# Two attention loops of a two-block kernel: operands split once and loaded through SyncE, masks added on VectorE, and the units put in another order

## The reference, cut to what matters

```python
# window attention: 16 heads in 4 groups that share keys and values, head width 64, 128-query blocks
s_win = jnp.where(valid, einsum(qb, kb) * scale, NEG_INF)     # keys within +-128
s_ctx = einsum(qb, k_ctx) * scale                             # 256 context keys
p = softmax(concat([sink, s_ctx, s_win]))[1:]                 # a sink logit per head
out = einsum(p, concat([v_ctx, vb]));   y = (out * silu(g)) @ w_out_c

# forgetting attention: 8 heads, causal, cum = cumsum(log_sigmoid(f))
s = einsum(q_blk, k) * scale + c_blk[..., None] - cum_k
out = einsum(softmax(where(mask, s, -inf)), v)

# beside it: causal depthwise convolution of 31 taps, then layer norm and silu
u = silu(layer_norm_2(causal_depthwise_conv(u, conv_w, conv_b), g, b))
```

## Time and profile before

| | us |
|---|---|
| median of 3 runs | 2823.35 (2822.56 to 2829.22) |
| profiled execution, its own time | 2825.2 |
| its span in the profile | 2823.4 |
| TensorE busy in the span | 2456.3 (87%) |
| VectorE, GpSimd, ScalarE busy | 1486.1, 1377.5, 879.9 |
| window attention, 883 to 1230 | 347 |
| forgetting attention, 1679 to 1885 | 206 |
| mean granted TensorE clock, share of full | 0.928 |

### The profile page before, as it was taken

One profiled execution on the slowest core, in us unless ns is written; L12 is line 12 of the kernel. 1 busy time (PEld: TensorE's weight loads), 2 busy tenths in 40 slices (PEclk: granted clock), 3 DMA queues, 4 the chain that ended last, 5 costly groups with the idle time before them and its releaser, 6 DMA issues. The chain is left out here.

```text
span 2823.4 us, 32941 instructions
## 1 busy us (share of the span) xinstructions
PE 2456.3 (87%) x11695; PEld 2025.6 (72%) x11695; DVE 1486.1 (53%) x2088; ACT 879.9 (31%) x1534; POOL 1377.5 (49%) x1348
## 2 busy tenths in 40 slices
PE   6799998988998999989778946578789999999996
PEld 2688886777887888877556735467567887888874
DVE  1715636565453888846879547663862222222236
ACT  3521112133014777743323346552341000000012
POOL 2445646552424656427557835346564453333350
PEclk9899999999997989989899978879899999999997
DMA  7345434322243223133232233315222221111121
GB/s 251 127 146 149 112 109 153 138 60 105 89 150 103 86 75 98 46 118 116 59 117 66 79 134 98 97 60 194 60 78 72 68 82 45 45 48 54 53 71 60
DMA packets 146129, 273.33 MB, mean 97 GB/s; under 512 B 16236, under 2 KB 50344, under 8 KB 144688
## 3 DMA queue, kind: packets, MB, share of 16 engines
q1 hardware_dynamic: 114208, 177.65, 20.8%
q10 hardware_dynamic: 31760, 93.57, 9.0%
HBM read 224.99 MB, written 46.17 MB: 96 GB/s over the span
## 5 line engine op out<-in xcount | busy, mean ns | idle before, releaser
L807 POOL TENSOR_SCALAR WH<-RAW 128x512 fp32r<-128x512 f32 (+1 forms) x470 | 345.7, 735 | 1017.7 <-PE PS L920 892.5
L918 PE MATMUL PS<-HXH,WH 128*128 128x512 f32 (+1 forms) x1904 | 762.0, 400 | 87.0 <-DVE XX L2170 23.1
L919 PE MATMUL PS<-HXL,WH 128*128 128x512 f32 (+1 forms) x1904 | 751.7, 395 | 0.0
L920 PE MATMUL PS<-HXH,WL 128*128 128x512 f32 (+1 forms) x1904 | 750.8, 394 | 0.0
L810 POOL TENSOR_TENSOR WL<-RAW,WH 128x512 fp32r<-128x512 f32 (+1 forms) x470 | 644.8, 1372 | 39.2
L918 PEld LDWEIGHTS PS<-HXH,WH 128*128 128x128 f32 (+1 forms) x1904 | 363.3, 191 | 177.0 <-DVE XX L2170 23.7
L919 PEld LDWEIGHTS PS<-HXL,WH 128*128 128x128 f32 (+1 forms) x1904 | 363.4, 191 | 79.1 <-issue 2.7
L920 PEld LDWEIGHTS PS<-HXH,WL 128*128 128x128 f32 (+1 forms) x1904 | 362.3, 190 | 79.4
L2209 DVE TENSOR_TENSOR TM<-PS,TM 128x512 f32<-128x512 f32 x44 | 28.4, 686 | 378.7 <-ACT TM L1625 378.6
L1625 ACT ACTIVATE TM<-PS 128x512 f32<-128x512 f32 x44 | 23.9, 595 | 552.1 <-PE PS L920 552.1
L895 POOL TENSOR_SCALAR PB<-PB,RC 128x640 f32<-128x640 f32 (+1 forms) x128 | 99.7, 779 | 159.3 <-DVE RC L2400 159.1
(11 more groups left out here) (281 smaller groups left out, 4519.0 us busy)
## 6 DMA issues: line engine op xcount, KB each, us to landing
RAW<-in_ada_w SPq DMA_DIRECT2D x160, 256.0 KB, 2.7
RAW<-in_w_ffn_in SPq DMA_DIRECT2D x224, 128.0 KB, 2.1
RAW<-in_w_in_ab SPq DMA_DIRECT2D x88, 256.0 KB, 2.7
RAW<-in_w_in SPq DMA_DIRECT2D x56, 256.0 KB, 2.7
RAW<-in_w_ffn_out SPq DMA_DIRECT2D x52, 256.0 KB, 2.6
XR<-XX ACTq DMA_DIRECT2D x3, 4096.0 KB, 12.1
XX<-XR ACTq DMA_DIRECT2D x3, 4096.0 KB, 14.0
RAW<-in_w_in_c SPq DMA_DIRECT2D x40, 256.0 KB, 2.7
```

The source lines that it names most:

```text
L807: g.tensor_scalar(WH[:, sw, 0:m], RAW[:, r, 0:m], 1.0, 0.0, ALU.mult, ALU.add).then_inc(gpsimd_done, 1)
L918: mm(out, wh, xh, start=first, stop=False, **kw)
L919: mm(out, wh, xl, start=False, stop=False, **kw)
L920: return mm(out, wl, xh, start=False, stop=last, **kw)
```

## The change: what it does

1. **Operands are split once, where they are made.** After a `q` projection of the first block VectorE writes the rotated queries to `RX`, ScalarE the high part, VectorE the low part, and ScalarE's queue stores both (`QXD`, two stores where there was one). The same is done for `q2`, `k2` and `v2` with `SPH` and `SPL`; there a PSUM bank is now free when VectorE's low part has been taken, not after ScalarE's copy. VectorE's list has these subtractions between the parts of the convolution.
2. **SyncE loads the parts ready for use** in `beside(n)`, between the slots of its list: per block of window attention eight loads of queries (2 MB, each half of the partitions written twice) and one of the gate; per head of the forgetting attention six loads of queries and keys (1.5 MB), the decay row (0.5 MB) and the values (0.5 MB). All `prep` functions go.
3. **Window masks on VectorE.** The extreme and the mask are one instruction (scores plus mask to `PB`, line 2454), ScalarE's exponential works in place on `PB`, the two mask matmuls go, the sink's column is written once per group and head, and scores wait for the extreme of unit u-2, not for the exponential.
4. **Another order.** `AT` says at which unit a tile is transposed, `PV_AT`, `OTT_AT` and `OTA_AT` when a step's product, copy and sum run; VectorE takes the low parts a unit later, ahead of that unit's extreme, and the reciprocal after it; GpSimd's `ada_tile` stands after heads 3 and 0 and not after 0 and 1.
5. **The layer norm's tail** (reciprocal in four pieces, multiplications, `Silu`, store) moves into `attf`, between its units 5 and 22.

```diff
+CONV_TAIL = (5, 7, 9, 11, 13, 15, 17, 19, 22)
+        AT = {"c": {5: [5, 5, 6, 6, 7], 4: [5, 6, 7, 7]},
+              "f": {8: [5, 5, 5, 5, 6, 6, 7, 7], 4: [6, 7, 7, 8]}}
+        PV_AT, OTT_AT, OTA_AT = {"c": 9, "f": 9}, {"c": 11, "f": 9}, {"c": 13, "f": 13}
...
+            def load_q(b):
...
+                if b >= 2:
+                    sp.wait_ge(products_done, upto("sc", "c", 16 * (b - 1) - 1))
+                for x in range(2):
+                    for half in range(2):
+                        src = QXD[x][64 * half:64 * half + 64, 2 * kv:2 * kv + 2, hf * HALF:(hf + 1) * HALF]
+                        for o_ in (slice(0, 64), slice(64, P)):
+                            sp.dma_start(QS[b % 2][x][o_, half:4:2, :].bitcast(F32), src).then_inc(rq_loaded[b % 2], 16)
...
+            def load_v(hd):
+                if hd >= 2:
+                    sp.wait_ge(products_done, upto("pv", "f", 2 * hd - 3))
+                else:
+                    for j in range(4):
+                        sp.wait_ge(split_stored[j], upto("sps", ("v2", "h1"), j))
...
+                if f == 0:
+                    load_v(0)
+                    load_qk(1)
+                    load_nb(1)
+                    load_v(1)
+                if 4 <= f < 32 and f % 4 == 2 and f // 4 < 7:
+                    load_qk(f // 4 + 1)
+                    load_nb(f // 4 + 1)
...
             for n, (kind, src, _) in enumerate(SLOTS):
+                beside(n)
...
                             if u >= 2:
-                                pe.wait_ge(scalar_done, upto("exp", "c", u - 2))
-                            pe.wait_ge(vector_done, upto("qs", s // 4, h // 2))
+                                pe.wait_ge(vector_done, upto("mx", "c", u - 2))
+                            pe.wait_ge(rq_loaded[(s // 4) % 2], upto("rql", s // 4))
...
+                            if i == 0 or (h < 2 and i in (1, 7)):
+                                sink = (PS[:, sb, p0 * P + 127:p0 * P + 128] if h < 2 else PS[:, sb + 1, 256:257])
+                                ins = mm(sink, ONF[0:1, :], NSK[0:1, hd:hd + 1], start=True, stop=True)
...
+                        for z, ti in tiles.get(u - 1, []):
+                            low(z, ti)
...
+                            v.tensor_tensor_reduce(out=PB[s % 2][:, h, lo + x:641 + x], in0=src, in1=mask[:, x:641 - lo + x],
+                                                   scale=1.0, scalar=3e38, op0=ALU.add, op1=ALU.min,
+                                                   accum_out=MX[s % 2][:, h:h + 1]).then_inc(vector_done, 1)
...
                 elif kind == "attf":
                     tiles = spread("f")
+                    for j in range(4):
+                        dve.wait_ge(split_stored[j], upto("sps", ("v2", "h1"), j))
+                    dve.wait_ge(scalar_done, upto("csd"))
```

532 lines of the change are left out of this document (270 added, 262 removed).

## The result

The changed kernel takes **2682.82 us** (median of 4, 2680.55 to 2686.06), the kernel before, run beside it, 2822.95 (2820.26 to 2829.22): ratio 0.9501, 95% interval 0.9482 to 0.9521. The forecast was 2740, range 2705 to 2778. The sign was right; the gain was 140 us and not 83. The profiled execution has a span of 2679.2 us, 144.2 less than before's 2823.4.

What follows compares the result with a forecast made beforehand. It took window attention as bound by TensorE's work and forgetting attention by a chain through ScalarE and VectorE. Terms 40 + 8 + 17 + 18 = 83 us off 2825.2 gave 2742, median 2740, range 2705 to 2778.

Steps and rivals of the forecast that it cites:

- The new order costs no instruction. [...] Both are inside the 300.: Window attention: 340 falls to 300 us, a term of 40 (0 to 70), the new order's effect included.
- VectorE busy at 81%, its share today: Window attention: VectorE's busy share stays as before in the 300 us taken for the changed loop.
- So the first loop is bound by TensorE's work: Window attention before the change: TensorE busy 93%, its summed work 336 of 340 us.
- TensorE's need: Window attention changed: TensorE's work alone takes 270 us at clock 0.92, the loop's lower bound.
- The 188 us: Forgetting attention from its first unit: 206 falls to 188 us, a term of 18, between 0 and 46.
- Ahead of window attention: Before the first window scores: queries lie ready, so scores start at about 875; term 8 us, bounds 5 and 9.
- the sign that I gave, 4 us: Ahead of window attention: first scores come 4 us after the last gate store starts, not 9.
- Convolution stage and the hole behind it: Before forgetting attention: the hole shrinks, less 2.4 us of convolution delay; term 17 us, bounds 12 and 24.
- VectorE's bound is reached: Both attention loops: window attention at 270, forgetting attention at 160, kernel 2682 us; chance 0.06.
- Only the holes close: Both loops are paced by round trips and stay as long; gain 8 + 17 = 25 us, kernel 2798; chance 0.08.
- The clock, the other side: Window attention: thinner TensorE work lowers the granted clock; at 0.60 the kernel takes 2853 us; chance 0.04.
- SyncE's list: Both loops: loads hold back modulation weights, 13 bursts of GpSimd waiting lose 139 us, kernel 2879; chance 0.03.

Runs made afterwards that it cites:

- e11: Changed kernel with the whole order undone and window scores waiting for the exponential again: 2743.98 us, window attention 299.7, forgetting attention 190.2.
- e1: Changed kernel with its new order (fourth part) undone: 2744.03 us, window attention 299.2, forgetting attention 192.3.
- e7: Changed kernel with order and scores' wait undone, TensorE's removed window work back, layer norm's tail ahead of forgetting attention: 2750.66 us, window attention 310.5.
- e2: Changed kernel with TensorE's removed window work put back (two identity matmuls and the sink in every unit): 2712.34 us, window attention 306.6.
- b1: Kernel before, without its mask matmuls and with sinks only in each group's first block: 2812.23 us, window attention 333.3.
- e10: Changed kernel with only the tables of units for tiles, products, copies and sums undone: 2722.34 us, window attention 284.4, forgetting attention 187.9.
- e4: Changed kernel with two modulation weight pieces loaded ahead of the nine loads at forgetting attention's start: 2673.09 us, forgetting attention 156.4.
- e5: Changed kernel with the layer norm's tail back ahead of forgetting attention: 2668.41 us, forgetting attention 147.6.
- e6: Changed kernel with 64 idle VectorE subtractions added in window attention, four in a row: 2752.04 us, window attention 340.3.
- e9: Changed kernel with GpSimd's modulation weights after heads 0 and 1 again in both loops: 2687.19 us, window attention 270.1, forgetting attention 169.2.
- e16: Changed kernel with two weight pieces first, tail ahead of forgetting attention, and modulation weights after heads 0 and 1 in window attention only: 2658.55 us.

## Why the prediction was wrong, point by point

**Window attention, the step that failed: "The new order costs no instruction. [...] Both are inside the 300."** The 300 were set between 270 and 340 by shares of work, the order was to be inside them, and so it was priced at nothing of its own. Work alone gives 299.7 (`e11`); that this meets the 300 to a microsecond is luck. The order and the earlier release of the scores are worth 22 to 25 us more (`e1`, `e11`), where TensorE's work is out; with it in, 4 (`e7` against `e2`). The same belief stands in "VectorE busy at 81%, its share today": that share was itself made by VectorE waiting 24.5 us for exponentials and 23.8 for high parts. With the work out and the old order those waits are 42.5 and 17.5 (`e11`), changed 13.4 and 24.2: 22.4 us less, and the loop 22.7. The wait that I had in a row, for high parts, is the one that did not shrink.

**"So the first loop is bound by TensorE's work" was wrong too.** `b1` took 57 us of that work and gained 7. As the waits read, the loop was paced by VectorE and ScalarE waiting for each other (in `b1` ScalarE waits 68.7 us for extremes, VectorE 23.7 and 24.1 for exponentials and high parts), with TensorE nearly as long beside it. Of the 63 us, 29 came with the splits that left VectorE and ScalarE (`e7`), and 34 with TensorE's masks and sinks, order and wait, more than half of these only because both were changed. The 270 us that I gave as "TensorE's need" used the clock of 0.92; with 0.97 it is 256.

**Forgetting attention: the same step, and a term mis-sized.** The 188 us were counted in a stretch of 206; first to last scores, 201.6, the term of 18 makes it 183.6. With the old order it takes 190.2 (`e11`), so the work taken gave 11 and not 18. The order gives 27 more, 24 of which hang on the tables (`e10`). GpSimd's wait for `RAW` came as forecast, 12.3 us, not 8; `e4` shows that the loop pays for it. The tail was counted as a gain of the change. The hole ahead of the loop closed by 23.9 us because loading, copying and subtracting went: with the tail put back ahead of it the scores start as early (`e5`, 7.5 us and not 8.2). Moving the tail into the loop was a loss of 14, since ahead it would have filled GpSimd's wait, and inside its `Silu` hold TensorE up.

**Ahead of window attention** 8 us, measured 8.6: right. The first scores start 0.1 us after the last store of the gate; the sign that I gave, 4 us, did not fit my own term, which puts them at 875, 0.6 after it. **Convolution stage and the hole behind it** 17, measured 26.6. The delay of 2.4 us does not show: from the last window scores to the column sums it takes 419.4 us, 418.2 to 422.0 in other executions with the same instructions there, and 422.1 before. The landing of `v2`'s stores, which I had put at the end of the hole (first extreme 1662 of the old count), was not what ended last, by half a microsecond: the first extreme came 10.7 us behind the start of the column sums' matmuls, right behind the square root and its scores. So the upper bound, 24, was also too low. What lay on the path was the issue of the stores, until 1572.1, ahead of the square root in ScalarE's list. That short runs would bring the term nearer to 12 did not come; the low parts' stores landed 4.8 us behind their issue (median), and no run shows their rate.

**The rivals.** *VectorE's bound is reached* gave 2682, which is what came, and the reason it named, that each engine works on another unit, fits the runs. That the numbers meet is partly luck: its terms 70, 8, 17 and 46 were 65.8, 8.6, 26.6 and 38.1, and 5.1 us came from the rest of the kernel. I gave it 0.06, against it VectorE's share today, the quantity the change alters. In forgetting attention its picture is wrong: VectorE is busy 114 of 169 us there, 68%, as before. *Only the holes close* fell by `e11`. *The clock, the other side*: the granted clock rose, 0.92 to 0.97 and 0.84 to 0.88. It fell where VectorE held TensorE up: 0.86 in `e6`, 0.78 in the forgetting attention of `e1`. The Trainium skill, "TensorE: Matmul & The Clock Gate", section "A second HAM failure mode: psum-queue depth-cycling", says that small pauses between groups of matmuls make the clock swing. Those two stretches agree with it; that thinner work brings it about does not follow, since in window attention TensorE is busy 89% of the time in the changed kernel and 93% in the one before, and the clock rose. *SyncE's list*: one wait for `RAW`, 12.3 us, instead of 13 bursts.

**The range** missed because both loops came near their best bounds, 65.8 of 70 and 38.1 of 46, and I had called that unlikely. I treated the terms as if each fell by itself; one cause, the order, moved both.

## What to carry to other kernels

A busy share of 93% says that an engine has little air, not that taking its work away helps: look at who waits for whom between the other engines first. Do not price an order at nothing because it adds no instruction. The waits of before say that it can matter, here 24 us each for exponential and high part, but they are no price: once work was taken out the first had grown to 42.5 us, and only then was the order worth 23. Where two engines hand a value back and forth, put what needs the other's answer behind what the other is waiting for. And before work is moved out of a hole, ask who else uses the hole, here the loads, and what a block of it does to the chain inside the loop, here 7 us.

## What the runs showed of the hardware

**A VectorE instruction with two SBUF inputs and a GpSimd instruction that reads SBUF hold each other up.** In the changed kernel's window attention (timeline):

```profile
957.68 2.21 DVE L1993 TENSOR_TENSOR OT<-OT,GT 128x1024 f32<-128x1024 f32 x1
958.79 1.77 POOL L1010 TENSOR_SCALAR PB<-PB,RC 128x640 f32<-128x640 f32 x1
```

The scaling ends 0.67 us behind the end of VectorE's instruction with two SBUF inputs, as if it had started with that end: 959.89 + 0.81 = 960.70 against 960.56, 0.81 being its length alone. Over the loop the gate's multiplication and the scaling, changed kernel first, then `e9` (ns least/median/most):

```profile
L1993 DVE TENSOR_TENSOR OT<-OT,GT x8: 1224/2047/2211, 923.0 to 1157.1; 128x1024 f32<-128x1024 f32 x8
```

```profile
L1010 POOL TENSOR_SCALAR PB<-PB,RC x128: 690/802/1786, 876.3 to 1149.1; 128x640 f32<-128x640 f32 x96, 128x512 f32<-128x512 f32 x32
```

```profile
L1993 DVE TENSOR_TENSOR OT<-OT,GT x8: 1224/1226/1227, 925.5 to 1154.2; 128x1024 f32<-128x1024 f32 x8
```

```profile
L1010 POOL TENSOR_SCALAR PB<-PB,RC x128: 689/800/818, 877.4 to 1146.2; 128x640 f32<-128x640 f32 x96, 128x512 f32<-128x512 f32 x32
```

With the modulation weights after heads 0 and 1 the scaling no longer meets the gate's multiplication: none takes over 818 ns, the multiplication always 1.23 us, and the loop is 7 us shorter. It now meets a piece of the modulation weights (1531 ns at most, 695 in the changed kernel), for which TensorE does not wait. `e16` shows the same rows. That this is the whole cause of the 7 us is inferred; no run moved the multiplication alone. The idle subtractions show it from VectorE's side: 682 ns at least and 1670 at most in `e6`. An extreme with a mask, one input from PSUM and one from SBUF, shows none of it: 803 to 829 ns for 128 x 641 elements in the changed kernel. The Trainium skill, "SBUF — State Buffer", section "Who interferes with whom", says that a VectorE instruction with two SBUF inputs contends with a GpSimd instruction that reads SBUF; the rows agree.

**The clock** rose in the changed kernel, but not because TensorE has less work: `b1` has less and 0.88, `e2` and `e7` have the work back and 0.95 and 0.96, against 0.92 before and 0.97 changed. Part of the rise is at the start, 0.50 in the first 20 us before and 0.74 in the changed kernel; what brings the rest stays open. A kernel's granted clock is thus no constant to carry from before into a sum: 0.92 and 0.97 differ by 14 us over this loop's 248 us at full clock.
